# The down projection of an FFN as seven block products: two of three parts, weights in chunks of four k tiles, block sums moved to GpSimd

## The chip, the core and the metric

The kernel runs on one core of one Trainium2 chip. A time is the device time of one launch in microseconds (us); the smaller, the better. TensorE (PE) multiplies into PSUM, VectorE (DVE) and ScalarE (ACT) work on SBUF and PSUM, GpSimd (POOL) on SBUF, and SyncE (SP) issues the loads. The engines run side by side and wait for one another on semaphores.

## What is computed

A trunk of two layers on 512 tokens of width 1024, all in float32. Each layer has an FFN, a mixing part (three branches), and a second FFN; the change touches only the four FFNs.

```python
def swiglu(h, w_gate, w_up, w_down):
    return (jax.nn.silu(h @ w_gate) * (h @ w_up)) @ w_down
...
for i in range(DEPTH):        # DEPTH = 2, D_MODEL = 1024, D_FF = 2816, SEQ = 512
    x = x + 0.5 * swiglu(rms_norm(x, ffn1_norm[i]), ffn1_w_gate[i], ffn1_w_up[i], ffn1_w_down[i])
    ...                       # attention, gating and pooling branches, output projection
    x = x + 0.5 * swiglu(rms_norm(x, ffn2_norm[i]), ffn2_w_gate[i], ffn2_w_up[i], ffn2_w_down[i])
return rms_norm(x, final_norm)
```

## The kernel before

**Precision.** Each float32 operand is split into a rounded part "hi" (written by ACT) and the rest "lo" (written by DVE, a subtraction). A product is three matmuls: hi by hi, hi by lo, lo by hi.

**Units.** Weights come in units of 256 columns. A gate or up unit has the eight k tiles of D_MODEL. A plain unit is `columns`: 2 column halves by 8 k tiles by 3 matmuls, 48 matmuls of 512 tokens. Gate and up units alternate; two of them make a pair, which gives two k tiles of the activation. An FFN has 11 pairs, cut into three parts (`PART_PAIRS`): 3, 4 and 4 pairs. After the pairs of a part come its four down units (`D_PAIRS`), which multiply the part's activation by 256 columns of `w_down` and are added to the residual `xT`.

**Seven products.** In parts 2 and 3 a gate or up unit is `unit7`: token halves, weight column halves and k halves form 2 by 2 blocks, and seven products of block sums take the place of eight (Strassen's method in Winograd's form). Each product is 4 k tiles by 3 matmuls of 256 tokens, so a unit has 84 matmuls of 256. The sums of weight blocks (`t_sum`) are made by DVE in `t_sums`, ACT rounds them (`hi_t123`, `hi_rest`), DVE makes their lo parts (`lo_first`, `lo_rest`). The results of the seven products are joined by DVE from the PSUM tensors `psum` and `side` in three steps (four instructions). The six gate and up units of part 1 and all twelve down units are plain.

**Order.** Each engine runs a program written out by hand; the waits are on semaphores. PE works without a pause from unit to unit; ACT and DVE prepare the weights of one or two units ahead, between the evacuations. `act_lo_part` writes the lo part of a pair's activation, and PE waits for it pair by pair: the first down unit of a part has the last pair's two k tiles last (`need_act`).

## Time and profile before

| what | value |
|---|---|
| time, median of 3 runs | 2287.54 us (2286.88 to 2287.69) |
| span of the profiled execution, first to last instruction | 2285.9 us |
| median less span: what lies around the instructions | 1.6 us |
| PE busy | 100% of the span |
| DVE busy | 67% |
| ACT busy | 37% |
| GpSimd busy | 1% |
| mean granted TensorE clock | 0.999 of full speed |

The page gives busy time of each engine, the chain of work that ended last, and what an engine waited for. Matmuls are pipelined: one has a duration longer than the distance to the next, so their cost is read from the distance of starts. DVE and ACT durations include a fixed part that overlaps slightly with the next instruction.

### The profile page before, as it was taken

How to read it: one execution, taken by the hardware profiler on the slowest of the kernel's cores; microseconds unless marked ns; L12 is line 12 of the kernel's file. 1: busy time of each engine (PE TensorE's matmuls, PEld its weight loads, DVE VectorE, ACT ScalarE, POOL GpSimd, SP SyncE). 2: the span in 40 equal slices, each digit the busy share in tenths (PEclk: the TensorE clock that was granted, in tenths of full speed). 3: DMA queues.
4: the chain of work that ended last, by engine and by line, in shares of the span. 5: the costliest groups of instructions: out<-in, count | busy, mean ns of one | idle time of the engine just before them, and what ended most of it. 6: DMA issues, size and time to landing. Idle time of an engine off the chain costs nothing.

```text
span 2285.9 us, 31530 instructions
## 1 busy us (share of the span) xinstructions
PE 2275.0 (100%) x13549; PEld 1998.1 (87%) x13549; DVE 1529.1 (67%) x1721; ACT 849.6 (37%) x937; POOL 30.8 (1%) x70
## 2 busy tenths in 40 slices
PE   9999999999999999999999999999999999999998
PEld 7898998888888888989888989889888888899897
DVE  6895977455544568959668959665554355698694
ACT  5343433323522334424334434332244224344342
POOL 5000000000000000000000000000000000000000
PEclk9999999999999999999999999999999999999999
DMA  5324233322222423323223333332212333233232
GB/s 162 97 93 129 75 111 115 93 74 66 79 83 87 129 85 100 111 92 112 94 90 112 94 111 94 110 115 84 83 51 79 96 118 99 79 108 128 75 113 72
DMA packets 231393, 222.68 MB, mean 97 GB/s; under 512 B 4208, under 2 KB 229600, under 8 KB 231264
## 3 DMA queue, kind: packets, MB, share of 16 engines
q1 hardware_dynamic: 225744, 215.29, 30.0%
q10 hardware_dynamic: 5520, 5.51, 0.7%
q8 instruction: 100, 1.64, 0.3%
q14 instruction: 29, 0.24, 0.0%
HBM read 218.69 MB, written 2.10 MB: 97 GB/s over the span
## 4 chain that ended last, share of the span: by engine, by line
PE 99%; DVE 1%; ACT 0%; issue 0%; DVEq 0%; POOL 0%; POOLq 0%
PE psum L571 56%; PE psum L623 16%; PE side L623 12%; PE psum L837 6%; PE psum L771 2%; PE side L571 1%; PE psum L583 1%; PE side L894 1%; PE side L854 1%; PE side L874 0%; PE side L879 0%; PE side L781 0%; PE side L753 0%; PE side L862 0%; PE psum L698 0%; PE side L792 0%
## 5 line engine op out<-in xcount | busy, mean ns | idle before, releaser
L571 PE MATMUL psum<-h_hi,w_hi 128*128 128x512 f32 x944 | 369.5, 391 | 0.2 <-DVE wide L1446 0.2
L571 PE MATMUL psum<-h_hi,w_lo 128*128 128x512 f32 x944 | 367.4, 389 | 0.0
L571 PE MATMUL psum<-h_lo,w_hi 128*128 128x512 f32 x944 | 367.3, 389 | 0.0
L1424 DVE TENSOR_TENSOR w_lo<-raw,w_hi 128x2048 fp32r<-128x2048 f32 (+2 forms) x127 | 248.4, 1956 | 100.2 <-ACT w_hi L970 99.4
L970 ACT ACTIVATE w_hi<-raw 128x2048 fp32r<-128x2048 f32 (+2 forms) x127 | 208.6, 1642 | 246.9 <-PE psum L571 219.8
L623 PE MATMUL psum<-s_hi,hi 128*128 128x256 f32 x1024 | 289.8, 283 | 0.0
L623 PE MATMUL psum<-s_lo,hi 128*128 128x256 f32 x1024 | 289.8, 283 | 0.0
L571 PE MATMUL psum<-act_hi,w_lo 128*128 128x512 f32 x704 | 273.9, 389 | 0.0
L1068 ACT ACTIVATE hi<-t_sum 128x1536 fp32r<-128x1536 f32 (+1 forms) x128 | 134.2, 1055 | 264.7 <-DVE t_sum L1608 264.7
L571 PE MATMUL psum<-act_hi,w_hi 128*128 128x512 f32 x576 | 224.1, 389 | 0.0
L571 PE MATMUL psum<-act_lo,w_hi 128*128 128x512 f32 x576 | 224.1, 389 | 0.0
L623 PE MATMUL psum<-s_hi,t_lo 128*128 128x256 f32 x768 | 217.3, 283 | 0.0
L623 PE MATMUL side<-s_lo,hi 128*128 128x256 f32 x768 | 217.3, 283 | 0.0
L623 PE MATMUL side<-s_hi,hi 128*128 128x256 f32 x768 | 217.3, 283 | 0.0
L571 PEld LDWEIGHTS psum<-h_hi,w_hi 128*128 128x128 f32 x944 | 177.2, 188 | 37.8 <-issue 0.7
L571 PEld LDWEIGHTS psum<-h_lo,w_hi 128*128 128x128 f32 x944 | 177.2, 188 | 37.3 <-issue 0.7
L571 PEld LDWEIGHTS psum<-h_hi,w_lo 128*128 128x128 f32 x944 | 177.2, 188 | 36.8
L623 PEld LDWEIGHTS psum<-s_hi,hi 128*128 128x128 f32 x1024 | 196.6, 192 | 0.0
L623 PEld LDWEIGHTS psum<-s_lo,hi 128*128 128x128 f32 x1024 | 196.6, 192 | 0.0
L1489 DVE SCALAR_TENSOR_TENSOR xT<-psum,xT 128x1024 f32<-128x1024 f32 x53 | 64.9, 1224 | 139.6 <-PE psum L571 139.3
L571 PEld LDWEIGHTS psum<-act_hi,w_lo 128*128 128x128 f32 x704 | 132.1, 188 | 27.4
L623 PEld LDWEIGHTS side<-s_hi,hi 128*128 128x128 f32 x768 | 147.4, 192 | 0.3
(272 smaller groups left out, 4342.2 us busy)
## 6 DMA issues: line engine op xcount, KB each, us to landing
raw<-in_ffn_w_up_dram SPq DMA_DIRECT2D x44, 1024.0 KB, 5.4
raw<-in_ffn_w_gate_dram SPq DMA_DIRECT2D x43, 1024.0 KB, 5.4
raw<-in_w_in_dram SPq DMA_DIRECT2D x42, 1024.0 KB, 5.3
raw<-in_ffn_w_down_dram SPq DMA_DIRECT2D x32, 1024.0 KB, 5.2
raw<-in_ffn_w_down_dram SPq DMA_DIRECT2D x16, 768.0 KB, 4.5
raw<-in_w_in_dram SPq DMA_DIRECT2D x24, 512.0 KB, 4.2
raw<-in_w_out_dram SPq DMA_DIRECT2D x8, 1024.0 KB, 5.3
raw<-in_w_proj_b_dram SPq DMA_DIRECT2D x8, 512.0 KB, 3.5
```

The costliest lines, as they stand in the source:

```text
L571: mm = nc.tensor.matmul(dst[:, c * S:(c + 1) * S], l[:, a], r[:, b], start=first and k == ks[0] and n == 0, stop=last and k == ks[-1] and ...
L583: mm = nc.tensor.matmul(o, l[:, k * P:(k + 1) * P], r[:, k * S:(k + 1) * S], start=(k == 0 and n == 0), stop=(k == KD - 1 and n == 2))
L623: mm = nc.tensor.matmul(o[:, col:col + HALF], l(k), r[:, b], start=k == 0 and n == 0, stop=k == KH - 1 and n == 2)
L771: mm = nc.tensor.matmul(d, l[:, k * S + t * P:k * S + (t + 1) * P], r[:, b], start=(k == 0 and m == 0), stop=(k == KD - 1 and m == 2))
L837: mm = nc.tensor.matmul(psum[0][:, c * S:(c + 1) * S], l[:, k * UNIT_N + c * P:k * UNIT_N + (c + 1) * P], r[:, k * S:(k + 1) * S], start=( ...
L854: nc.tensor.matmul(outs[b][h * HQ:(h + 1) * HQ, col:col + k1 - k0], t[rows_of(b), q + h * HQ:q + (h + 1) * HQ], t[rows_of(b), k + k0:k + k ...
L894: mm = nc.tensor.matmul(side[1][rows_of(b), KEYS + q0:KEYS + q1], v[:, col:col + HEAD_DIM], pT[b][:, c0:c0 + q1 - q0], start=(m == 0), sto ...
L970: nc.scalar.activation(w_hi[s][:, 0:k * n], raw[s][:, 0:k * n], ACT.Copy).then_inc(hi_made, 1)
L1068: nc.scalar.activation(dst, src, ACT.Copy).then_inc(hi_made, 1)
L1424: nc.vector.tensor_tensor(w_lo[s][:, a], raw[s][:, a], w_hi[s][:, a].bitcast(F32), ALU.subtract).then_inc(split_made, 1)
L1489: i_ = nc.vector.scalar_tensor_tensor(x_, src, scale, x_, ALU.mult, ALU.add)
```

## The change

- The parts are 4, 4 and 3 pairs. The first six gate and up units stay plain. The other sixteen gate and up units and the eight down units of parts 1 and 2 are made as seven products (`seven`). The four down units of part 3 stay plain, now over six k tiles.
- The weights of a unit with seven products come in two chunks of four k tiles (512 KB each): 48 chunks an FFN, numbered 0 to 47. Chunks 0 to 3 are the last pair of part 1, 4 to 11 its down units, 12 to 27 the gate and up units of part 2, 28 to 35 its down units, 36 to 47 part 3. A chunk is 42 matmuls of 256 tokens; the second chunk of a unit adds to the first in PSUM. A down unit's two chunks stand in a row on PE: the first reads pairs 1 and 2 of the part, the second pairs 3 and 4.
- The block sums of the weights are made by GpSimd (`weight_sums`), two chunks ahead, behind the chunk that frees their buffer (three sets). GpSimd also makes the sums of the input (`input_sums`) and five of the eight block sums of a part's activation; DVE makes the last three (`act_sums`), when the last pair is there.
- DVE writes a pair's product into `ac_sum`; ACT rounds its seven blocks in groups, and DVE writes their lo parts in the same groups (`act_group`). PE waits for the three groups of pairs 1 and 2 before the first chunk of the first down unit, and for the three of pairs 3 and 4 before its second.
- A down unit is joined by DVE in four instructions and then added to `xT` from SBUF (before: one instruction from PSUM).

```diff
-    PART_PAIRS = ((0, 3), (3, 7), (7, 11))
-    PART_AT = (0, 10, 22)
+    PART_PAIRS = ((0, 4), (4, 8), (8, 11))
+    PART_AT = (0, 12, 24)
...
+    PLAIN = 6
...
+    CK = 4
+    CH = CK // 2
+    Q = CH * P
...
+            def weight_sums(f, q):
...
+                    after_chunk(pool, f, q - SETS)
+                after_loaded(pool, f, q)
+                t, b = t_sum[q % SETS], blocks(c_raw[q % RAWS])
+                nc.gpsimd.tensor_tensor(t[:, 0:2 * Q].rearrange("p (h k n) -> p h k n", h=2, n=P), b[:, :, :, 1, :],
+                                        b[:, 0].rearrange("p k c n -> p c k n"), ALU.subtract).then_inc(t_step, 1)
+                pool.wait_ge(t_step, 2 * (f * NC + q) + 1)
+                nc.gpsimd.tensor_tensor(tile7(t, T2_), tile7(t, T3_), b[:, 0, :, 0, :], ALU.add).then_inc(t_step, 1)
+                pool.wait_ge(t_step, 2 * (f * NC + q) + 2)
+                nc.gpsimd.tensor_tensor(tile7(t, T4_), b[:, 1, :, 0, :], tile7(t, T2_), ALU.subtract).then_inc(t_made, 1)
...
+            def seven(f, q, x_hi, x_lo, x_k, width, order):
...
+                pe.wait_ge(chunk_lo, 3 * (f * NC + q) + 2)
...
+                mm.then_inc(chunk_done if j == 0 else unit_done, 1)
...
+                for q, (n, j) in enumerate(CHUNKS):
...
+                    if down:
+                        if (n, j) == (PART_AT[p + 1] - D_PAIRS, 0):
+                            pe.wait_ge(ac_ready, 6 * (2 * f + p) + 3)
+                        if (n, j) == (PART_AT[p + 1] - D_PAIRS, 1):
+                            pe.wait_ge(ac_ready, 6 * (2 * f + p) + 6)
+                        seven(f, q, ac_hi[j], ac_lo[j], 0, CH, DOWN_ORDER)
...
+        LO_GROUPS = {0: ((0, 0, 0),), 1: ((0, 0, 1),), 2: ((0, 0, 2),), 4: ((0, 1, 0), (0, 1, 1), (0, 1, 2)),
+                     21: ((1, 0, 0),), 22: ((1, 0, 1),), 23: ((1, 0, 2),), 28: ((1, 1, 0), (1, 1, 1), (1, 1, 2))}
```

DVE's loop over the chunks, which sets the order of its work (`finish` joins the unit before; at the end of a part it also makes the product and the sums):

```diff
+                    pending = finish(*finished) if finished is not None else None
+                    finished = None
+                    if q + 2 < NC:
+                        chunk_lo_b(q + 2)
...
+                    if j == 1 and not down:
+                        dve.wait_ge(product_done, 6 * m + 3)
...
+                        take_first(m, s)
+                    if q + 2 < NC and j == 0:
+                        chunk_lo_t(q + 2)
+                    if j == 1 and not down:
+                        dve.wait_ge(product_done, 6 * m + 5)
+                        take_second(s)
+                    if q + 2 < NC and j == 1:
+                        chunk_lo_t(q + 2)
...
+                    for p_, j_, g_ in LO_GROUPS.get(q, ()):
+                        act_group(p_, j_, g_)
```

**DVE, behind the last up unit of a part.** Before, from the wait for the end of that unit (`unit_done`): joining, product, lo part, then the weights of the next down unit and its evacuation. L1576 is the lo part that PE waits for.

```order
L1670 TENSOR_TENSOR wide<-side,acc 128x512 [waits unit_done]
L1674 TENSOR_TENSOR wide<-wide 128x1024 [waits silu_made,side_evacuated1]
L1576 TENSOR_TENSOR act_lo<-wide,act_hi 128x1024 [waits act_hi_made]
L1636 TENSOR_TENSOR w_lo_57<-raw_74,w_hi_55 128x2048 [waits hi_made]
L1489 SCALAR_TENSOR_TENSOR xT<-psum,xT 128x1024 [waits unit_done]
```

Of the change, from the same wait: joining, product into `ac_sum`, three sums, the three lo instructions of the chunk after next (L1739, L1746, L1748), and the three groups (L1700) that PE waits for.

```order
L1777 TENSOR_TENSOR wide<-side,rstd 128x512 [waits unit_done]
L1675 TENSOR_TENSOR ac_sum_96<-wide 128x2x2x256 [waits silu_made,side_evacuated1]
L1685 TENSOR_TENSOR ac_sum_96<-ac_sum_96 128x512 [waits ac_pool,ac_made]
L1687 TENSOR_TENSOR ac_sum_96<-ac_sum_96 128x512 [waits ac_step]
L1689 TENSOR_TENSOR ac_sum_96<-ac_sum_96 128x512 [waits ac_step]
L1739 TENSOR_TENSOR c_raw_lo_80<-c_raw_75,c_hi_90 128x4x128 [waits chunk_hi,t_made]
L1746 TENSOR_TENSOR t_lo_87<-t_sum_84,c_hi_90 128x1024 [waits chunk_hi]
L1748 TENSOR_TENSOR c_raw_lo_80<-c_raw_75,c_hi_90 128x2x128
L1700 TENSOR_TENSOR ac_lo_98<-ac_sum_96,ac_hi_94 128x1024 [waits ac_hi_made,ac_summed]
L1700 TENSOR_TENSOR ac_lo_98<-ac_sum_96,ac_hi_94 128x1024 [waits ac_hi_made]
L1700 TENSOR_TENSOR ac_lo_98<-ac_sum_96,ac_hi_94 128x1536 [waits ac_hi_made]
```

Three instructions stood between the end of the unit and the last value that PE needs; now eleven do.

**PE, where it waits for the last pair of a part.** Before, in the first down unit of part 2, the wait for the last pair stands behind 36 of the unit's 48 matmuls.

```order
L571 MATMUL psum<-act_hi,w_lo_56 128x512
L571 MATMUL psum<-act_hi,hi_d 128x512 [waits act_ready]
L571 MATMUL psum<-act_lo,hi_d 128x512
```

Of the change, at the start of chunk 5, the second of the first down unit of part 1; the 42 matmuls of chunk 4 stand ahead of it.

```order
L764 MATMUL side<-ac_hi_93,c_raw_lo_83 128x256
L764 MATMUL side<-ac_hi_94,c_hi_92 128x256 [waits chunk_lo,ac_ready]
L764 MATMUL side<-ac_lo_98,c_hi_92 128x256
```

The wait moved from behind 36 matmuls of 512 to behind 42 of 256.

**GpSimd.** Before, it has after the masks of the start only two instructions in the whole program.

```order
L522 AFFINE_SELECT masks<-masks 128x128 [waits mask_step]
L530 AFFINE_SELECT w_sT<-w_sT 128x512 [waits side_evacuated1] x2
```

Of the change, the sums of chunks 2 and 3 and the one activation sum behind them: three instructions a chunk, each behind the one before, the first behind PE's end of an earlier chunk (`chunk_done` or `unit_done`).

```order
L618 TENSOR_TENSOR t_sum_86<-c_raw_76 128x512 [waits chunk_loaded2,split_made]
L621 TENSOR_TENSOR t_sum_86<-t_sum_86,c_raw_76 128x256 [waits t_step]
L623 TENSOR_TENSOR t_sum_86<-c_raw_76,t_sum_86 128x256 [waits t_step]
L618 TENSOR_TENSOR t_sum_84<-c_raw_77 128x512 [waits chunk_loaded3,chunk_done]
L621 TENSOR_TENSOR t_sum_84<-t_sum_84,c_raw_77 128x256 [waits t_step]
L623 TENSOR_TENSOR t_sum_84<-c_raw_77,t_sum_84 128x256 [waits t_step]
L630 TENSOR_TENSOR ac_sum_96<-ac_sum_96 128x512 [waits ac_made]
```

GpSimd had nothing to do in an FFN; now it has 144 such instructions for weights in each, and every chunk passes through it before ACT and DVE.

## Rows read from the trace of the kernel before

**Rows 1.** The page: span, then busy time, share and instructions of engines

```profile
span 2285.9 us, 31530 instructions
PE 2275.0 (100%) x13549; PEld 1998.1 (87%) x13549; DVE 1529.1 (67%) x1721; ACT 849.6 (37%) x937; POOL 30.8 (1%) x70
```

**Rows 2.** The page: the chain that ended last, by engine

```profile
PE 99%; DVE 1%; ACT 0%; issue 0%; DVEq 0%; POOL 0%; POOLq 0%
```

**Rows 3.** All waits of PE: for whom, us in total, times, longest

```profile
PE psum L698 <- POOL ident L487: 1.7, 1, 1.7
PE side L598 <- DVE acc L1769: 1.3, 1, 1.3
PE psum L571 <- DVE wide L1446: 0.2, 1, 0.2
```

**Rows 4.** The chain in order of time: start us, us, instructions merged

```profile
114.35 5.76 PE psum L623 x48
124.43 5.76 PE psum L623 x48
...
193.55 43.55 PE psum L571 x192
```

**Rows 5.** Groups of DVE by form: busy us, mean ns, idle before

```profile
L1620 DVE TENSOR_TENSOR t_lo<-t_sum,hi 128x1536 fp32r<-128x1536 f32 x64 | 112.1, 1752 | 0.0
...
L1608 DVE TENSOR_TENSOR t_sum<-t_sum,raw 128x512 f32<-128x512 f32 x64 | 44.3, 692 | 2.2
...
L1670 DVE TENSOR_TENSOR wide<-side,acc 128x512 f32<-128x512 f32 x64 | 44.2, 691 | 14.7 <-PE side L623 13.1
L1663 DVE TENSOR_TENSOR acc<-psum,wide 128x512 f32<-128x512 f32 x64 | 43.9, 687 | 10.9 <-PE psum L623 10.3
...
L1674 DVE TENSOR_TENSOR wide<-wide 128x1024 f32<-128x1024 f32 x32 | 39.2, 1226 | 1.1
...
L1664 DVE TENSOR_TENSOR wide<-psum,acc 128x256 f32<-128x256 f32 x64 | 27.2, 424 | 2.2
```

**Rows 6.** Timeline of DVE from 35 us: start us, us, instruction

```profile
35.17 2.35 DVE L1446 TENSOR_TENSOR wide<-psum,rstd 128x1024 f32<-128x1024 f32 x2
```

**Rows 7.** Timeline of GpSimd, the masks at the start: start us, us, instructions merged

```profile
19.41 2.95 POOL L516 TENSOR_SCALAR_AFFINE_SELECT masks<-masks 128x128 bf16<-128x128 bf16 x3
...
24.20 3.35 POOL L516 TENSOR_SCALAR_AFFINE_SELECT masks<-masks 128x128 bf16<-128x128 bf16 x3 [0.50 <-POOL masks L509]
...
34.01 1.09 POOL L516 TENSOR_SCALAR_AFFINE_SELECT masks<-masks 128x128 bf16<-128x128 bf16 x3
...
375.50 0.64 POOL L530 TENSOR_SCALAR_AFFINE_SELECT w_sT<-w_sT 128x512 f32<-128x512 f32 x1 [339.96 <-ACT w_sT L1237]
```

**Rows 8.** Timeline of DVE over the first two of these stretches

```profile
19.02 2.39 DVE L1424 TENSOR_TENSOR w_lo<-raw,w_hi 128x2048 fp32r<-128x2048 f32 x1 [0.56 <-ACT w_hi L970]
23.65 3.74 DVE L1768 TENSOR_TENSOR squares<-squares,squares 128x1024 f32<-128x1024 f32 x3 [2.24 <-ACT squares L991]
```

**Rows 9.** Lines L516 and L1424 alone: duration ns min/median/max

```profile
L516 POOL TENSOR_SCALAR_AFFINE_SELECT masks<-masks x12: 294/294/2152, 19.4 to 34.8; 128x128 bf16<-128x128 bf16 x12
...
L1424 DVE TENSOR_TENSOR w_lo<-raw,w_hi x127: 681/2291/2390, 19.0 to 2011.9; 128x2048 fp32r<-128x2048 f32 x83, 128x1024 fp32r<-128x1024 f32 x20, 128x1536 fp32r<-128x1536 f32 x16, 128x512 fp32r<-128x512 f32 x8
```

**Rows 10.** PE's last instructions, from the timeline

```profile
2277.60 0.60 PE L939 MATMUL psum<-ident,xT 128*128 128x128 f32 x4
```

**Rows 11.** Windows of the end: busy us of engines, PEclk, DMA share, GB/s

```profile
2279.00:2280.00 1.00, 0.00 (x0) 0.00 (x0) 1.00 (x2) 0.69 (x1) 0.00 (x0) 1.00 0.46 174
2280.00:2281.00 1.00, 0.00 (x0) 0.00 (x0) 1.00 (x2) 0.69 (x1) 0.00 (x0) 0.87 1.02 375
2281.00:2282.00 1.00, 0.00 (x0) 0.00 (x0) 0.21 (x1) 0.00 (x0) 0.00 (x0) 0.50 1.01 377
```

**Rows 12.** The page: issues of loads, KB each, median us from issue to landing

```profile
raw<-in_w_in_dram SPq DMA_DIRECT2D x24, 512.0 KB, 4.2
```

**Rows 13.** A group of ACT by form: busy us, mean ns, idle before

```profile
L1091 ACT ACTIVATE act_hi<-wide 128x1024 fp32r<-128x1024 f32 x32 | 34.0, 1061 | 89.7 <-DVE wide L1674 89.7
```

More of the change, by code:

```diff
@@ new lines, in act_sums @@
+            def act_sums(f, p, j, which):
+                t, made = ac_sum[j], 8 * f + 4 * p + 2 * j
+                for o, x1, x2, op, step in which:
+                    pool.wait_ge(ac_made, made + step)
+                    nc.gpsimd.tensor_tensor(quarter(t, o, 0, CH, CH), quarter(t, x1, 0, CH, CH), quarter(t, x2, 0, CH, CH),
+                                            op).then_inc(ac_pool, 1)
+                    act_sums.n += 1
+                    pool.wait_ge(ac_pool, act_sums.n)
+            act_sums.n = 0
@@ new lines, in need_act @@
+                def need_act(k):
+                    if k % 2 == 0:
+                        pe.wait_ge(act_ready, counts["act"].next())
+                for d in range(D_PAIRS):
+                    pe.wait_ge(split_made, counts["unit"].next())
+                    slot = DOWN_SLOTS[d]
+                    columns(begin(d % 2), (w_hi[slot], w_lo[slot]), act_hi, act_lo, range(DOWN_K[2][1] - DOWN_K[2][0]), True, True,
+                            need=need_act if d == 0 else None, halves=True).then_inc(unit_done, 1)
@@ L1047, in inner @@
                     counts["unit"].next()
[L1048 removed]
+                    if i < PLAIN // 2 - 1:
+                        split()
+                    else:
+                        chunk_hi_b(0)
+                        chunk_hi_t(0)
                     counts["unit"].next()
@@ L1101, in split_d, with down_split @@
+                def down_split(d):
+                    k = DOWN_K[2][1] - DOWN_K[2][0]
+                    r = DOWN_SLOTS[d]
+                    act.wait_ge(raw_loaded[r], counts[f"raw{r}"].next(16))
                     act.wait_ge(unit_done, counts["unit"].now(2))
                     a = slice(0, k * UNIT_N)
-                    hi(w[:, a], (raw7 if d == 1 else raw[r])[:, a])
-                for i in range(PART_PAIRS[0][1]):
+                    nc.scalar.activation(w_hi[r][:, a], raw[r][:, a], ACT.Copy).then_inc(hi_made, 1)
@@ new lines, in ffn @@
+                act.wait_ge(act_made, 3 * f + pending + 1)
+                nc.scalar.activation(pair(act_hi, pending), us[:, :], ACT.Copy).then_inc(act_hi_made, 1)
+                for d in range(D_PAIRS):
+                    if d < D_PAIRS - 1:
+                        down_split(d + 1)
+                    elif not last or layer < DEPTH - 1:
+                        split()
+                    counts["unit"].next()
+                    if last and layer == DEPTH - 1:
+                        last_residual(d, d % 2)
+                    else:
+                        residual(gain, d, d % 2)
@@ new lines, in ffn @@
+                    for p_, j_, g_ in LO_GROUPS.get(q, ()):
+                        act_group(p_, j_, g_)
+                    if j == 1:
+                        finished = ((n, p, i, down, s), m)
+                clear_acc()
+                act_lo_part(finish(*finished))
+                for d in range(D_PAIRS):
+                    if d < D_PAIRS - 1:
+                        down_split(d + 1)
+                    elif not last or layer < DEPTH - 1:
+                        split()
+                    if not (d == D_PAIRS - 1 and last and layer == DEPTH - 1):
+                        done()
+                    if last and layer == DEPTH - 1:
+                        last_residual(0.5, d, d % 2)
+                    else:
+                        residual(0.5, gain, d, d % 2)
```

743 lines of the change are left out of this document (378 added, 365 removed).

## Prediction

> **What bounds the kernel now.** I read the page first: PE is busy for the whole span of 2285.9 us, DVE for 67%, GpSimd for 1% [rows 1]. A busy PE alone proves nothing, so the chain of what ended last comes next: 99% of it is PE [rows 2]. The waits settle it: in the whole program PE waited three times, 3.2 us in all, and 0.2 us of that inside an FFN [rows 3]. So in the FFNs the time is the number of matmuls by their distance, and every wait that the change gives to PE is paid in full. The distances come from the chain in order of time. A unit of 84 matmuls of 256 tokens is followed 10.08 us later by the same place of the next: 120 ns a matmul. 192 matmuls of 512 tokens take 43.55 us: 226.8 ns a matmul [rows 4].
>
> **PE's own work.** A plain down unit over eight k tiles is 48 matmuls, 10.88 us; as seven products it is 84, 10.08 us: 0.80 us less, not an eighth, as a matmul of 256 costs more than half of one of 512. Per FFN the gate and up units stay as they are (six plain, sixteen of seven products). The down units had 22 k tiles by 4 units, 528 matmuls of 512; now they have 144 of those and 8 by 84 of 256. That is 384 by 226.8 ns (87.1 us) out, 672 by 120 ns (80.6 us) in: 6.4 us less an FFN, **25.6 us less** in four.
>
> **Where PE would wait: the second chunk of the first down unit.** Call T the end of the last up unit of a part. Before, PE had 36 matmuls of 512 (8.2 us) before it needed the last pair, and DVE needed three instructions. Now PE has one chunk, 42 by 120 ns = 5.04 us. DVE has in a row: joining 0.69, product 1.23, three sums 3 by 0.69, the lo parts of the chunk after next 0.69 + 1.23 + 0.42, the three groups 1.23 + 1.23 + 1.75 [rows 5]; there joining is L1670, the product and everything of 1024 is L1674, 512 from SBUF is L1608, 256 is L1664, 1536 is L1620. The sum is 10.5 us; instructions without a wait between them overlap by 0.1 us (two of 1.225 take 2.35 [rows 6]), which leaves 10.1. DVE isn't free at T either: it can take the fifth product only 12 matmuls before T (T - 1.44), the two instructions of that step last 0.69 + 0.42 (L1663, L1664), then L1746 and L1748 of another chunk follow (1.55), to T + 1.2. The groups are ready at T + 11.3: **PE waits 6.3 us** in part 2.
>
> In part 1 the same chain stands behind a backlog. DVE can't start on chunk 1 before the last plain unit ends (ACT's buffer for it waits for that). From there to the last group of pairs 3 and 4 it has 38 instructions: 13 of 1024 (15.9), 2 of 1536 (3.5), 9 of 512 in SBUF (6.2), 6 of 512 from PSUM (4.1), 8 of 256 (3.4), together 33.2, less about 20 overlaps of 0.1: 31.1 us. PE has five chunks, 25.2 us, ahead of its wait: **5.9 us** of waiting, if DVE never waits itself. The two make 12.2 us an FFN, 48.8 in four.
>
> **GpSimd against DVE.** The masks show what GpSimd does beside DVE. Three L516 take 1.09 us at 34.01, where DVE runs a reciprocal or reads PSUM, but 2.95 us at 19.41 and 3.35 us at 24.20 [rows 7]. There DVE runs instructions with two inputs in SBUF [rows 8]; one L516 took 2152 ns, not 294, and ended just behind DVE's, and that DVE instruction took 2390 ns, not the median 2291 [rows 9]. So the two take turns, whole instructions at a time, and the loser waits. Almost all that DVE does in a chunk has two inputs in SBUF, and so have all of GpSimd's sums. No row has GpSimd with two inputs. The nearest: one input of 512 float32 takes 0.64 us, of 128 elements 0.29, so 0.9 ns an element [rows 7, 9]. A chunk's sums have 1024 elements: 0.9 us of holding at that rate, 1.8 at twice it. I take the upper, as each element needs two operands, and 2.0 with the hand-overs. Behind T two chunks' sums fall into DVE's chain (one starts at T, one a chunk later): 4.0 us, less 0.7 beside joining, which reads PSUM: 3.3. In part 1 four chunks' sums and one of the activation do (8.9), of which DVE's nine instructions from PSUM and its waits for ACT can hide half: 4. Together 7.3 us an FFN, **29 in four**; from below 1.3 and 0 (5 in four), from above 5 and 8 (52).
>
> The Trainium skill (GPSIMD Engine Reference, Performance versus the Vector engine) measured a two-input add of 2048 float32 on GpSimd at 4497 ns, 2.2 ns an element; by that a chunk's sums hold 2.25 us instead of 1.8, and the sum would be some 7 us higher. No row of this trace can confirm it.
>
> **The clock.** PE's last matmul starts at about 2278 us [rows 10], and the granted clock is 1.00 until 2280, 0.87 in the next us, then 0.50, that is 1.2 instead of 2.4 GHz [rows 11]. So an idle PE has the lower level within about 2.5 us, and a wait of 9 us ends in it. No row shows the way back: between nothing and a whole chunk at half rate (5 us lost). I take 2 us, eight times: **16**.
>
> **What costs nothing.** Loads: 512 KB land in 4.2 us [rows 12], and a chunk is asked for two chunks ahead; so they stay hidden. Behind the last up unit of part 3 the cover shrinks to 24 matmuls, 5.4 us; DVE needs 0.69 + 1.23, ACT 1.06 [rows 13], DVE 1.23 again, some 4.5 with DVE free at T - 0.3: it just fits, and would cost what it lacks if DVE is late. In the steady stretches DVE has per chunk 2.4 us of lo parts, 1.3 of joining and up to 0.6 for products, GpSimd about 2.6, against 5.04: covered, with little to spare.
>
> **Sum.** The profiled span of 2285.9 and the 1.6 around it give the median of 2287.5. 2287.5 - 25.6 + 48.8 + 29 + 16 = **2356 us**, 3% slower.
>
> **The rivals.**
> - *The cover is enough* (faster). ACT and DVE have all but the last pair ready ahead, PE never waits, 2287.5 - 25.6 = 2262 us. For it: DVE has a third of its time free. Against: that third isn't behind T, where eleven instructions of 10.5 us stand against 5.04. It decides at the point where the last group ends before T + 5.04, which needs five microseconds of those instructions to be absent. Between it and the next, a total wait under 6.4 us an FFN would do. Chance 0.11, and 0.03 for landing at no change.
> - *Only DVE's chain* (slower, little). GpSimd's turns are short or fall into DVE's idle time, and the clock returns at once: 2287.5 - 25.6 + 48.8 = 2311, up to 2320. Chance 0.16.
> - *GpSimd and DVE fill every chunk.* DVE holds the SBUF inputs about 2.4 us a chunk, a quarter of a product (0.3) and in part 2 the groups; GpSimd 2.0. That is 4.7 of 5.04. If GpSimd's instructions cost half as much again, or each change of turns 0.1 us more, the loop needs 5.4 in all 192 chunks: 0.4 by 192 = 77 us on top, 2356 + 77 = 2433. For it: the doubled durations in rows 7. Against: PE stalls give slack back. The Trainium skill (SBUF — State Buffer, Who interferes with whom) has this as an exclusive lock for the whole instruction; the 2152 ns agree. Chance 0.12.
> - *As forecast*, 2320 to 2400: chance 0.58.
>
> **Numbers.** 2356. The low end is 48.8 and 5 for the turns with a free return of the clock, 2316, and some microseconds for instructions that I placed too late: 2306. The high end takes 52 for the turns and 40 for the clock: 2403. Outside are the fast rival and the saturated one. Slower by over 0.2% (4.6 us, about what a measurement can tell from no change) 0.86, same 0.03, faster 0.11.
>
> **What would show it.** The waits of PE in the changed kernel name L764 <- DVE `ac_lo` L1700, eight times, 6 to 13 us each, and little else. The lines of GpSimd show L618 over 1 us, with a spread up to DVE's durations. PEclk falls to half around these waits. The count of matmuls grows by 1152. The prediction is wrong if PE's waits for L1700 are under 3 us (then DVE gets there sooner than its rows say), or if they are small beside waits for `chunk_lo` (L1746, L1748) everywhere (then the turns decide), or if a matmul of 256 in `seven` isn't 120 ns apart.

## The result and the profile after

The changed kernel takes 2476.66 us (2476.28 to 2477.02, four runs) against 2287.31 us before: ratio 1.0828, 95% interval 1.0813 to 1.0844. It is 189 us slower; 2356 was forecast, with 2403 as the high end. The direction was right, the size was not, and the largest single term of the loss was one that the forecast had at nothing.

The page of the changed kernel: span, busy times, and the chain that ended last, by engine.

```profile
span 2474.7 us, 35503 instructions
...
PE 2302.9 (93%) x14701; PEld 2071.2 (84%) x14701; DVE 1811.4 (73%) x1945; ACT 958.7 (39%) x1253; POOL 900.4 (36%) x702
...
PE 64%; DVE 21%; issue 6%; POOL 5%; ACT 4%; DVEq 0%; POOLq 0%; ACTq 0%
```

Against [rows 1] and [rows 2]: 1152 matmuls more, as counted, but the chain is PE for 64% only, where it was 99%. All waits of PE (for whom, us in total, times, longest):

```profile
PE side L764 <- DVE ac_lo L1700: 93.9, 12, 11.5
PE side L764 <- DVE t_lo L1746: 65.5, 44, 3.2
PE psum L817 <- POOL ident L551: 1.7, 1, 1.7
PE side L726 <- DVE acc L1897: 1.0, 1, 1.0
PE psum L699 <- DVE wide L1553: 0.2, 1, 0.2
```

The first row is the wait that was forecast, twelve times instead of eight: twice in each FFN in the second chunk of a part's first down unit, and once more at chunk 4, where PE waits some 2 us for the groups of pairs 1 and 2. The second is the surprise: 44 waits of 3.2 us at most, for the lo part of a chunk's block sums. Before there were three waits in all [rows 3].

What the preparing engines take, groups by form (busy us, mean ns, idle before), first DVE and then GpSimd:

```profile
L1746 DVE TENSOR_TENSOR t_lo<-t_sum,c_hi 128x1024 fp32r<-128x1024 f32 x192 | 281.3, 1465 | 61.4 <-ACT c_hi L1197 61.4
L1739 DVE TENSOR_TENSOR c_raw_lo<-c_raw,c_hi 128x512 fp32r<-128x512 f32 x192 | 224.0, 1167 | 31.4 <-POOL t_sum L623 30.5 <-ACT c_hi L1193 0.8
...
L1748 DVE TENSOR_TENSOR c_raw_lo<-c_raw,c_hi 128x256 fp32r<-128x256 f32 x192 | 171.0, 891 | 0.0
L1772 DVE TENSOR_TENSOR rstd<-psum,wide 128x512 f32<-128x512 f32 x96 | 66.4, 692 | 6.5 <-PE psum L764 3.3
...
L618 POOL TENSOR_TENSOR t_sum<-c_raw 128x512 f32<-128x512 f32 x192 | 315.5, 1643 | 365.0 <-PE side L764 355.9 <-issue 7.2
L623 POOL TENSOR_TENSOR t_sum<-c_raw,t_sum 128x256 f32<-128x256 f32 x192 | 228.3, 1189 | 15.1
L621 POOL TENSOR_TENSOR t_sum<-t_sum,c_raw 128x256 f32<-128x256 f32 x192 | 200.3, 1043 | 15.1
```

DVE's three lo instructions of a chunk take 3.52 us in the mean, where DVE's instructions of 1024, 512 and 256 columns took 1.23, 0.69 and 0.42 before [rows 5]: 1.19 us more. The 512 columns that read PSUM, 692 ns, are no longer than before. GpSimd's three sums take 3.88 us.

Where the time goes in the first FFN, in five stretches: chunks 0 to 2, 3 to 6 (into the down units of part 1), 7 to 22, 23 to 30 (the same at part 2), 31 to 47. Windows of the changed kernel: length, then busy us of PE, PEld, DVE, ACT and GpSimd (instructions), PEclk, DMA share, GB/s.

```profile
80.80:98.90 18.10, 15.35 (x126) 15.14 (x126) 18.03 (x16) 10.36 (x15) 16.86 (x13) 1.00 0.36 113
98.90:136.70 37.80, 25.91 (x168) 25.54 (x169) 30.50 (x34) 12.63 (x18) 12.34 (x11) 0.78 0.14 44
136.70:223.20 86.50, 81.86 (x675) 80.87 (x673) 79.19 (x83) 35.74 (x59) 65.53 (x52) 1.00 0.36 104
223.20:284.20 61.00, 44.77 (x336) 43.85 (x337) 52.35 (x56) 23.87 (x35) 32.21 (x26) 0.89 0.19 61
284.20:374.90 90.70, 86.72 (x715) 85.77 (x714) 84.11 (x90) 37.51 (x60) 57.76 (x45) 1.00 0.31 94
```

Read the lengths against 5.04 us a chunk, which is 15.1, 20.2, 80.6, 40.3 and 85.7. The two stretches around a boundary lose 17.6 and 20.7 us, the three others 3.0, 5.9 and 5.0. Of the 3.0, 2.9 us are the wait that ends the stretch, before the first matmul of chunk 3, and of the 5.9, 3.3 us are the wait before chunk 23. In chunks 7 to 22 DVE is busy for 79.19 of 86.5 us: 4.95 us a chunk against PE's 5.04. DVE's 73% on the page is an average; here it has hardly any room left.

### The profile page after: what moved, and what is told of

It is laid out like the page before. It is cut to its first block, busy times and chain, and to the rows that moved or that the text cites. A ratio compares the mean times of both kernels' runs of the same rounds, so it can differ in the third digit from the quotient of the medians.

```text
span 2474.7 us, 35503 instructions
## 1 busy us (share of the span) xinstructions
PE 2302.9 (93%) x14701; PEld 2071.2 (84%) x14701; DVE 1811.4 (73%) x1945; ACT 958.7 (39%) x1253; POOL 900.4 (36%) x702
## 4 chain that ended last, share of the span: by engine, by line
PE 64%; DVE 21%; issue 6%; POOL 5%; ACT 4%; DVEq 0%; POOLq 0%; ACTq 0%
PE psum L699 36%; PE psum L764 9%; PE side L764 7%; DVE t_lo L1746 5%; PE psum L956 5%; DVE c_raw_lo L1739 3%; DVE c_raw_lo L1748 3%; DVE ac_lo L1700 3%; PE psum L890 2%; POOL t_sum L618 2%; DVE rstd L1772 2%; DVE wide L1767 1%; DVE wide L1777 1%; POOL t_sum L621 1%; ACT c_hi L1197 1%
## 5 line engine op out<-in xcount | busy, mean ns | idle before, releaser
L618 POOL TENSOR_TENSOR t_sum<-c_raw 128x512 f32<-128x512 f32 x192 | 315.5, 1643 | 365.0 <-PE side L764 355.9
L1746 DVE TENSOR_TENSOR t_lo<-t_sum,c_hi 128x1024 fp32r<-128x1024 f32 x192 | 281.3, 1465 | 61.4 <-ACT c_hi L1197 61.4
L1197 ACT ACTIVATE c_hi<-t_sum 128x1024 fp32r<-128x1024 f32 x192 | 202.4, 1054 | 318.1 <-POOL t_sum L623 317.8
L1531 DVE TENSOR_TENSOR w_lo<-raw,w_hi 128x2048 fp32r<-128x2048 f32 (+1 forms) x111 | 228.3, 2057 | 102.6 <-ACT w_hi L1090 102.3
L764 PE MATMUL psum<-s_hi,c_hi 128*128 128x256 f32 x1024 | 295.0, 288 | 0.0
L764 PE MATMUL psum<-s_lo,c_hi 128*128 128x256 f32 x1024 | 294.9, 288 | 0.0
L764 PE MATMUL side<-s_hi,c_hi 128*128 128x256 f32 x768 | 224.6, 292 | 66.7 <-DVE t_lo L1746 65.5
L1739 DVE TENSOR_TENSOR c_raw_lo<-c_raw,c_hi 128x512 fp32r<-128x512 f32 x192 | 224.0, 1167 | 31.4 <-POOL t_sum L623 30.5
L623 POOL TENSOR_TENSOR t_sum<-c_raw,t_sum 128x256 f32<-128x256 f32 x192 | 228.3, 1189 | 15.1
L764 PE MATMUL side<-s_lo,c_hi 128*128 128x256 f32 x768 | 218.7, 285 | 0.0
L621 POOL TENSOR_TENSOR t_sum<-t_sum,c_raw 128x256 f32<-128x256 f32 x192 | 200.3, 1043 | 15.1
L764 PE MATMUL side<-ac_hi,c_hi 128*128 128x256 f32 x384 | 115.2, 300 | 94.3 <-DVE ac_lo L1700 93.9
```

The lines of the kernel that those rows point to most:

```text
L618: nc.gpsimd.tensor_tensor(t[:, 0:2 * Q].rearrange("p (h k n) -> p h k n", h=2, n=P), b[:, :, :, 1, :], b[:, 0].rearrange("p k c n -> p c k ...
L621: nc.gpsimd.tensor_tensor(tile7(t, T2_), tile7(t, T3_), b[:, 0, :, 0, :], ALU.add).then_inc(t_step, 1)
L623: nc.gpsimd.tensor_tensor(tile7(t, T4_), b[:, 1, :, 0, :], tile7(t, T2_), ALU.subtract).then_inc(t_made, 1)
L764: mm = nc.tensor.matmul(outs[side_][:, col:col + HALF], l, r[:, a], start=j == 0 and bank not in cleared, stop=j == 1 and k == CH - 1 and ...
L1197: nc.scalar.activation(c_hi[q % SETS][:, 0:4 * Q], t_sum[q % SETS][:, :], ACT.Copy).then_inc(chunk_hi, 1)
L1531: nc.vector.tensor_tensor(w_lo[s][:, a], raw[s][:, a], w_hi[s][:, a].bitcast(F32), ALU.subtract).then_inc(split_made, 1)
```

## The experiments

All times are compared with 2476.7 (the changed kernel) and 2287.4 to 2287.5 (before, in each group of runs). A time without a ratio or a range is that of a single run. Where GpSimd's weight sums are replaced, the block sums aren't computed.

### Take GpSimd's sums away

**w_short** and **w_long**: memsets, which read nothing, in place of the three sums.

```diff
-                nc.gpsimd.tensor_tensor(t[:, 0:2 * Q].rearrange("p (h k n) -> p h k n", h=2, n=P), b[:, :, :, 1, :],
-                                        b[:, 0].rearrange("p k c n -> p c k n"), ALU.subtract).then_inc(t_step, 1)
+                nc.gpsimd.memset(t[:, :], 1.0).then_inc(t_step, 1)
...
-                nc.gpsimd.tensor_tensor(tile7(t, T2_), tile7(t, T3_), b[:, 0, :, 0, :], ALU.add).then_inc(t_step, 1)
+                nc.gpsimd.memset(t[:, 0:1], 1.0).then_inc(t_step, 1)     # w_long: t[:, :]
...
-                nc.gpsimd.tensor_tensor(tile7(t, T4_), b[:, 1, :, 0, :], tile7(t, T2_), ALU.subtract).then_inc(t_made, 1)
+                nc.gpsimd.memset(t[:, 0:1], 1.0).then_inc(t_made, 1)     # w_long: t[:, :]
```

> GpSimd's three weight sums of a chunk are left out: in their place it writes constants, 1024 columns once and one column twice, and reads nothing (the output is not the reference's). Theory of turns (GpSimd and VectorE take turns at instructions that read SBUF, and GpSimd's 2.7 us a chunk lengthens VectorE's): VectorE's L1746, L1739 and L1748 return to 1.22, 0.69 and 0.42 us, the waits for chunk_lo in the steady stretches vanish, and the two waits of a part's first down unit shrink to about 6 us each: 2287.5 - 25.6 + 49 + 16 for the clock, 2315 to 2345 us. Rival, latency (the sums simply come too late to ScalarE and VectorE): also near 2330, as the sums are short here.

Measured: 2349.9, a little above the range.

> As the run before, but GpSimd writes 1024 columns of constants three times a chunk, about 2.9 us, as long as its real sums last when nothing disturbs them (2.7 us), still without reading SBUF. Theory of turns: as the short one, 2315 to 2350 us, with VectorE's lo parts at their lone durations. Rival, latency: the sums' length is what delays the chain, so 2430 to 2480 us, as the changed kernel.

Measured: 2364.1, 14 us over the range of the turns and 66 under that of the rival. So 127 of the 189 us go with the sums, and most of them even where GpSimd is busy 2.9 us a chunk, so long as it reads nothing. What is left has the forecast shape. Windows of w_short over the stretches 3 to 6, 7 to 22 and 23 to 30:

```profile
95.60:128.10 32.50, 22.53 (x170) 22.15 (x169) 25.54 (x33) 12.73 (x18) 4.60 (x12) 0.84 0.21 65
128.10:208.80 80.70, 80.70 (x675) 80.70 (x674) 63.67 (x85) 36.75 (x59) 24.77 (x52) 1.00 0.36 105
208.80:258.40 49.60, 42.19 (x337) 41.81 (x337) 41.19 (x54) 24.20 (x35) 10.87 (x25) 0.93 0.28 86
```

The steady stretch is at PE's pace, 80.7 us, and DVE has 3.98 us a chunk. The stretches around the boundaries still lose 12.3 and 9.3 us. In PE's timeline the waits (18.0) and slower matmuls (3.7) of an FFN add up to 21.7 us here, 86.8 in four; 2349.9 less that is 2263.1. So **PE's own work is what was forecast, 2262**.

### Give the sums to DVE, or share them

**sums_on_dve** moves the three sums into DVE's program, ahead of the lo parts of the same chunk.

```diff
                     if q + 2 < NC:
+                        weight_sums(q + 2)       # on DVE; none on GpSimd
                         chunk_lo_b(q + 2)
```

> The weights' block sums of every chunk are made by VectorE itself (0.69 + 0.42 + 0.42 us a chunk), all else as in the changed kernel. Theory of turns: GpSimd's 2.7 us a chunk cost VectorE more than making the sums would; VectorE then has about 5.1 us of work in a chunk of 5.04, so it is just full: 2262 + 60 for the two boundaries + 16 for the clock + 20 to 40, 2350 to 2385 us, faster than the changed kernel by 4 to 5%, still slower than before. Rival (VectorE's load decides, and GpSimd took work off it): slower than the changed kernel, above 2490 us.

Measured: 2511.2, ratio 1.0979 (1.0961 to 1.0998): worse than the change, and my expectation was wrong. The rival was right. Groups of DVE by form show why:

```profile
L1755 DVE TENSOR_TENSOR t_lo<-t_sum,c_hi 128x1024 fp32r<-128x1024 f32 x192 | 234.6, 1222 | 51.8 <-ACT c_hi L1193 51.7
...
L1748 DVE TENSOR_TENSOR c_raw_lo<-c_raw,c_hi 128x512 fp32r<-128x512 f32 x192 | 136.7, 712 | 6.3
L1738 DVE TENSOR_TENSOR t_sum<-c_raw 128x512 f32<-128x512 f32 x192 | 131.3, 684 | 0.0
L1740 DVE TENSOR_TENSOR t_sum<-t_sum,c_raw 128x256 f32<-128x256 f32 x192 | 97.2, 507 | 6.7
L1741 DVE TENSOR_TENSOR t_sum<-c_raw,t_sum 128x256 f32<-128x256 f32 x192 | 85.5, 445 | 6.6
```

The lo parts are back at 1222 and 712 ns, and so the 1.19 us are gone, but the sums bring 0.684 + 0.507 + 0.445 = 1.64 us. The order also has a gap, since the sums that ACT rounds are made just before: in the stretch below DVE waits 0.4 us for ACT (start us, us, instruction, idle before). Over all chunks these gaps add up to 51.8 us; the changed kernel has 61.4 at the same instruction, so they don't explain the difference.

```profile
156.48 0.68 DVE L1738 TENSOR_TENSOR t_sum<-c_raw 128x512 f32<-128x512 f32 x1
...
158.12 0.69 DVE L1748 TENSOR_TENSOR c_raw_lo<-c_raw,c_hi 128x512 fp32r<-128x512 f32 x1
159.21 1.23 DVE L1755 TENSOR_TENSOR t_lo<-t_sum,c_hi 128x1024 fp32r<-128x1024 f32 x1 [0.40 <-ACT c_hi L1193]
...
160.69 0.69 DVE L1738 TENSOR_TENSOR t_sum<-c_raw 128x512 f32<-128x512 f32 x1
```

From L1738 to the next L1738 it is 4.21 us for a chunk, before any joining of products. The window of chunks 7 to 22 has DVE busy 86.49 of 92.8 us, 5.41 a chunk, over PE's 5.04:

```profile
133.60:226.40 92.80, 84.97 (x675) 83.89 (x674) 86.49 (x131) 36.35 (x60) 5.90 (x4) 0.96 0.32 91
```

**sums_shared** leaves the sum of 512 on GpSimd and gives DVE the two of 256.

```diff
+                        rest_sums(q + 2)         # DVE: T2 and T4; GpSimd: T3 and T1 only
                         chunk_lo_b(q + 2)
```

> The changed kernel, but of a chunk's three sums GpSimd makes only the first (512 columns), and DVE the two of 256 ones, ahead of the chunk's lo parts, all computed. Until the sums are ready it now takes GpSimd about 1.5 us and DVE 0.95, where it took GpSimd 3.88. If GpSimd's lateness were the cause, this is a gain of 30 to 60 us: 2415 to 2445. If the sum of DVE's work decides: it gets 0.95 us more in each chunk and loses about half of the 1.19 us of lengthening, so its three lo instructions and sums take about 3.8 us where they took 3.52 (and 3.97 where DVE made all sums, 2511): 2485 to 2505.

Measured: 2531.7, ratio 1.1070 (1.1051 to 1.1088), above both guesses. Freeing GpSimd of half its sums gains nothing; it has the added DVE work and still a part of the lengthening. DVE's total on the page goes the same way in these three kernels, which compute everything: busy 1811.4, 1863.6 and 1883.9 us for 2476.7, 2511.2 and 2531.7. It is no measure by itself: the kernels with another order, below, have the changed kernel's total and are faster.

### Change the order

**two_first** runs the first two down units after a part as first, first, second, second chunk; **groups_first** puts the act groups of pairs 3 and 4 ahead of the next chunk's sums on ACT and DVE.

```diff
-            CHUNKS += [(n + d, j) for d in range(D_PAIRS) for j in range(2)]
+            CHUNKS += [(n, 0), (n + 1, 0), (n, 1), (n + 1, 1)]
+            CHUNKS += [(n + d, j) for d in range(2, D_PAIRS) for j in range(2)]
```
```diff
+                    if q in (4, 28):             # on DVE; on ACT ahead of chunk_hi_t in the same way
+                        for p_, j_, g_ in LO_GROUPS[q]:
+                            act_group(p_, j_, g_)
                     if q + 2 < NC:
                         chunk_lo_b(q + 2)
```

> The first chunks of a part's first two down units stand ahead of their second ones, so TensorE has 10.08 us instead of 5.04 before it needs pairs 3 and 4. If the boundary chain is VectorE's work behind the last up unit, each of the eight waits there shrinks by 5 us: 40 us less, 2430 to 2440 us. If that chain is fed by something that also moves (GpSimd's or ScalarE's work for later chunks), the gain is under 20 us.

Measured: 2458.6, ratio 1.0746 (1.0728 to 1.0764): 18 us, not 40, and so under the 20 of the second guess. PE's waits for `ac_lo` fell from 93.9 to 69.9 us only.

> At the two boundaries ScalarE and VectorE make the three groups of pairs 3 and 4 before the parts of the chunk after next, instead of behind them. In the changed kernel L1739, L1746 and L1748 stand there with 3.5 us in the mean (2.3 alone). If the boundary waits are this chain in VectorE's order, they shrink by 2.3 to 3.5 us each, 18 to 28 us in all: 2448 to 2460 us. If they are set by the three sums or by GpSimd, nothing changes: 2477 us.

Measured: 2460.2, ratio 1.0759 (1.0741 to 1.0777): 16 us, at the lower edge of the first guess. DVE has the same total in it, 1811.9 us.

**all_three** is these two edits and the sums on DVE; **both_orders** is the two edits alone, and **short_both_orders** has the memsets of w_short besides.

> Sums on VectorE, two first chunks ahead, and the groups first, together. If the three costs are separate and add up: 2365 less 40 for the cover less 18 for the order, about 2305 to 2325 us, near the kernel before. If VectorE's load is the bound in the steady stretches, the boundary gains are partly eaten there: 2330 to 2360 us.

Measured: 2484.5, ratio 1.0862 (1.0844 to 1.0881). A miss by over 120 us; it has the sums on DVE, which cost more than the orders gave, and against **sums_on_dve** the two orders are worth 27 us.

> The changed kernel with both reorderings of before together: the first two down units after a part take turns by chunks (their first chunks, then their second), and at that place ACT and DVE round the act groups before the weight sums of the chunk two ahead. Each alone took 18 and 16 us off 2476.7. If the two shorten different waits, about 2442. If both only let DVE's queue be shorter at the same place (that DVE has as much to do there as TensorE is what is waited for, whatever the order), 2448 to 2462: a reordering removes no DVE work.

Measured: 2451.2 (2444.8 to 2456.8), ratio 1.0724 (1.0706 to 1.0742): 25 of the 34 that they gave apart. The four runs are 12 us apart, so that the 25 is less certain than the figures of the other kernels.

> As both_orders, and GpSimd's three sums of a weight chunk are replaced by one memset of the chunk's 1024 columns and two of one column, as in w_short: the weights' block sums are not computed. w_short alone took 2349.9, with 21.7 us in each FFN (87 in all) of wait and lowered clock, nearly all of it at the two boundaries after a part; without that 87 it would be 2263, the 25.6 us under the kernel before that TensorE's products should save. If the boundary's wait is the act groups standing late in DVE's queue, the two reorderings now help more, as DVE has room: 2285 to 2315. If the wait there is DVE's own amount of work, 2325 to 2345.

Measured: 2304.2. With GpSimd's reads gone the same two edits are worth 46 us, with them 25. So at a boundary the order is worth more once DVE has room. From the distances of PE's matmuls the loss is then 42 us in four FFNs; 2304.2 - 42 is again 2262.

### Separate DVE's length from GpSimd's

**t_lo_set** keeps GpSimd's sums and makes `t_lo` a memset on DVE. **more_dve_work** and **some_dve_work** are w_short with three or two additions of 256 columns of constants a chunk. **gpsimd_long** has four memsets on GpSimd, **gpsimd_long_dve_more** those and DVE's three additions. **hi_in_halves** is the real kernel with ACT's rounding of the sums cut in two.

```diff
-                    nc.vector.tensor_tensor(t_lo[q % SETS][:, :], t_sum[q % SETS][:, :], w[:, 0:4 * Q].bitcast(F32),
-                                            ALU.subtract).then_inc(chunk_lo, 1)
+                    nc.vector.memset(t_lo[q % SETS][:, :].bitcast(F32), 0.0).then_inc(chunk_lo, 1)      # t_lo_set
```
```diff
+                    more = [nc.vector.tensor_tensor(spare[i]..., some, some, ALU.add) for i in range(3)]   # more_dve_work
```
```diff
+                    act.wait_ge(t_step, 2 * (f * NC + q) + 1)                                           # hi_in_halves
+                    nc.scalar.activation(c_hi[q % SETS][:, 0:2 * Q], t_sum[q % SETS][:, 0:2 * Q], ACT.Copy)
                     act.wait_ge(t_made, f * NC + q + 1)
-                    nc.scalar.activation(c_hi[q % SETS][:, 0:4 * Q], t_sum[q % SETS][:, :], ACT.Copy).then_inc(chunk_hi, 1)
+                    nc.scalar.activation(c_hi[q % SETS][:, 2 * Q:4 * Q], t_sum[q % SETS][:, 2 * Q:4 * Q], ACT.Copy).then_inc(chunk_hi, 1)
```

> The changed kernel, GpSimd's weight sums as they are, but DVE's t_lo (the fp32r remainder of a chunk's four sums, 1024 columns, a subtraction of 1.47 us in the mean) is a memset to zero of the same columns, which reads nothing: the remainders of the weights' sums are left out. If what TensorE waits for is the amount of DVE's work in a chunk (3.52 us in the three lo instructions, of it 1.19 us lengthening beside GpSimd), this takes away 0.4 to 1.2 us of it in every chunk (a memset of these columns may take 0.3 to 1.1 us): 2370 to 2430. If it is GpSimd's sums coming late (its three take 3.88 us in the mean, and ACT waits 318 us for them), the time stays over 2450.

Measured: 2403.5. That is 73 us less, though GpSimd still takes 3.8 us a chunk. DVE's memset took 0.91 us. Window over chunks 7 to 22:

```profile
131.90:213.40 81.50, 80.79 (x675) 80.58 (x673) 57.16 (x83) 36.21 (x59) 62.42 (x52) 1.00 0.36 104
```

With GpSimd's sums in place and reading, but DVE busy for 3.6 us a chunk, this stretch is within 0.8 us of PE's pace. The loss is around the boundaries: 35 us an FFN from the distances of PE's matmuls.

> As w_short (GpSimd sets the weights' sums by a memset and two columns, and is busy only 377 us in all; the block sums are not computed; 2349.9 us), but DVE does three more additions of 256 columns into unused memory after the first lo part of each chunk (43 of the 48 chunks of each FFN), a little over 1.1 us a chunk: about what DVE's three lo instructions are longer by beside GpSimd in the changed kernel (1.19 us). DVE's busy time then goes from 1577 to about 1780 to 1795 us, where the changed kernel has 1811. If the length of DVE's work is what costs, whoever lengthens it: 2430 to 2475. If it is that the sums come late from GpSimd, which is not so here: under 2380.

Measured: 2394.0. A miss: the added length costs 44 us, not 80 to 125. DVE's busy time grew to 1751.9, less than planned, as the three additions overlap and take 1.09 us together.

> As more_dve_work with two additions a chunk instead of three, about 0.75 us a chunk, DVE busy about 1715 us. If DVE's work costs in proportion, two thirds of the difference of more_dve_work to w_short: 2405 to 2430. If there is slack that the first part of it fills (DVE is idle a third of the time in w_short), less than half of the difference: 2365 to 2400.

Measured: 2378.4, 28 of the 44: two thirds, in proportion to the work added, as the first guess has it. The time lies in the range of the second because the 44 was smaller than thought.

> GpSimd's three weight sums of a chunk are replaced by four memsets of the chunk's 1024 columns, which read nothing and take 3.9 us together, as long as the sums in the changed kernel; the block sums are not computed, and DVE's instructions stay at their own length. w_long with three (2.9 us) took 2364.1, w_short with one 2349.9. If GpSimd's lateness costs by itself as in t_lo_set (2403.5), 2385 to 2410; if it costs only with DVE's length, under 2380.

Measured: 2371.0. GpSimd as late as in the changed kernel costs 21 us. This run is the nearest to the changed kernel that has no reads: GpSimd's instructions for a chunk last 3.82 us against 3.88, and DVE's program is the same. **So 106 of the 189 us (2476.7 less 2371.0) come from GpSimd reading instead of only writing.**

> As gpsimd_long, and DVE does the three additions of 256 columns a chunk of more_dve_work (1.07 us a chunk). So both engines take as long for a chunk as in the changed kernel, with no turns taken between them; the block sums are not computed. If the round of a chunk's buffers is what is too long (GpSimd 3.9 us, ACT 1.05, DVE's lo parts 3.5 beside ACT, its joining of products 2.5, some 10 us against 10.1 between two chunks), the two together cost more than their sum, and it comes near the changed kernel: 2450 to 2480. If they only add up, 2350 + 44 + what gpsimd_long has over 2350: 2415 to 2445. If the port does something more, the lower end or under it.

Measured: 2418.2. Both together cost 68, near 44 + 21. They add up; the theory of a buffer's round that is too long, with more than the sum, finds no support.

> The changed kernel, all computed, but ACT rounds a chunk's four sums in two instructions of 512 columns, the first when GpSimd's first sum is there, beside its other two, where one of 1024 (1.04 us) waited for all three. After the last sum ACT then takes about 0.6 us. If the round of a chunk's buffers is too long in the steady stretches, 0.4 us less of it is worth up to 0.4 us at each chunk that waits (some 12 of 48 in each FFN), with the clock that comes back after the shorter waits: 10 to 30 us, 2447 to 2467. If DVE's amount of work alone sets the pace, nothing: 2472 to 2480.

Measured: 2473.2 (2473.2 to 2474.1), ratio 1.0813 (1.0795 to 1.0831): 3.4 us for 0.4 us less in the round, where that theory expected 10 to 30.

The third stretch (chunks 7 to 22) of more_dve_work and of gpsimd_long_dve_more:

```profile
131.50:212.20 80.70, 80.70 (x675) 80.70 (x674) 78.20 (x131) 36.92 (x59) 24.46 (x52) 1.00 0.36 105
```
```profile
131.00:216.10 85.10, 81.14 (x674) 80.67 (x672) 78.51 (x131) 35.93 (x60) 67.25 (x69) 1.00 0.36 104
```

In the first, with DVE busy 4.89 us a chunk and all inputs early, PE never waits: a DVE that is 97% full can still be hidden. With the same DVE and GpSimd busy 67 us, 4.4 us are lost, nearly all at the starts of chunks 22 and 23. The changed kernel has 79.19 and 65.53 and loses 5.9.

What remains between 2418.2 and 2476.7 is 58 us. In it DVE's busy time goes from 1755.0 to 1811.4, 56 us more: the three additions stand only in 43 of an FFN's 48 chunks (20 chunks by 1.2 is 24 us), and in the changed kernel GpSimd's reads lengthen DVE's other two-input instructions as well. Two forms in the changed kernel, and the same in gpsimd_long_dve_more:

```profile
L1700 DVE TENSOR_TENSOR ac_lo<-ac_sum,ac_hi 128x1024 fp32r<-128x1024 f32 x32 | 51.9, 1641 | 0.0
L1800 DVE SCALAR_TENSOR_TENSOR xT<-wide,xT 128x1024 f32<-128x1024 f32 x32 | 47.0, 1468 | 1.1
```
```profile
L1809 DVE SCALAR_TENSOR_TENSOR xT<-wide,xT 128x1024 f32<-128x1024 f32 x32 | 39.2, 1226 | 1.1
...
L1703 DVE TENSOR_TENSOR ac_lo<-ac_sum,ac_hi 128x1024 fp32r<-128x1024 f32 x32 | 38.3, 1218 | 0.0
```

That these 56 us of DVE work are the 58 us of time is argued from the equal size, and not shown by a run of its own. The same argument fails elsewhere: **t_lo_set** and **gpsimd_long** have almost the same totals (DVE busy 1587.4 and 1576.7 us, GpSimd 884.2 and 890.0), and yet t_lo_set takes 33 us more. With GpSimd's reads its `ac_lo` groups of 1024 columns take 1600 ns instead of 1218, and PE waits 86.2 us for them instead of 70.9. So it matters which of DVE's instructions are lengthened. That GpSimd's turns fall unevenly on the chunks may be a part of the 58 us; these runs can't separate it.

## Why the prediction was wrong

**Right: PE's own work, -25.6.** Two runs come to it: 2349.9 - 86.8 = 2263 and 2304.2 - 42 = 2262. 120 ns a matmul of 256 held.

**Nearly right: the wait in the second chunk after a part.** PE's timeline in the first FFN (start us, us, instruction, idle before), at the second chunk of the first down unit of both parts:

```profile
124.25 0.58 PE L764 MATMUL side<-ac_hi,c_hi 128*128 128x256 f32 x1 [9.92 <-DVE ac_lo L1700]
...
272.33 0.58 PE L764 MATMUL side<-ac_hi,c_hi 128*128 128x256 f32 x1 [11.48 <-DVE ac_lo L1700]
```

From start to start of the matmuls, less 0.12 each, these are 10.1 and 11.6 us, 21.7 an FFN (in the third FFN 19.2), where DVE's chain (12.2) and GpSimd's turns (7.3) made 19.5. That the sum came so near is in part luck, as the split was less good: w_short, with few reads left on GpSimd, has 8.6 and 7.4 us there, 16.0, so the chain is 3.8 us longer than I counted and the turns are 5.7. DVE's timeline before the first of the two waits ends shows both, without a gap:

```profile
114.16 0.69 DVE L1685 TENSOR_TENSOR ac_sum<-ac_sum 128x512 f32<-128x512 f32 x1
114.88 1.64 DVE L1687 TENSOR_TENSOR ac_sum<-ac_sum 128x512 f32<-128x512 f32 x1
116.56 1.09 DVE L1689 TENSOR_TENSOR ac_sum<-ac_sum 128x512 f32<-128x512 f32 x1
117.57 1.21 DVE L1739 TENSOR_TENSOR c_raw_lo<-c_raw,c_hi 128x512 fp32r<-128x512 f32 x1
118.71 1.21 DVE L1746 TENSOR_TENSOR t_lo<-t_sum,c_hi 128x1024 fp32r<-128x1024 f32 x1
119.84 0.41 DVE L1748 TENSOR_TENSOR c_raw_lo<-c_raw,c_hi 128x256 fp32r<-128x256 f32 x1
120.17 4.02 DVE L1700 TENSOR_TENSOR ac_lo<-ac_sum,ac_hi 128x1024 fp32r<-128x1024 f32 x3
```

L1687, L1689 and L1739 have 512 columns like L1685 and take 1.64, 1.09 and 1.21 instead of 0.69, and just then GpSimd makes the sums of a chunk:

```profile
114.41 1.56 POOL L618 TENSOR_TENSOR t_sum<-c_raw 128x512 f32<-128x512 f32 x1 [3.99 <-PE side L764]
116.05 1.05 POOL L621 TENSOR_TENSOR t_sum<-t_sum,c_raw 128x256 f32<-128x256 f32 x1
117.18 1.05 POOL L623 TENSOR_TENSOR t_sum<-c_raw,t_sum 128x256 f32<-128x256 f32 x1
```

**Right: the clock, 2 us a boundary.** Windows over the end of the first of the waits and behind it (PEclk is the third number from the end):

```profile
120.00:124.00 4.00, 0.00 (x0) 0.00 (x0) 4.00 (x4) 0.00 (x0) 0.00 (x0) 0.50 0.00 0
124.00:126.00 2.00, 1.75 (x8) 1.76 (x9) 0.79 (x2) 0.07 (x1) 0.00 (x0) 0.50 0.00 0
126.00:128.00 2.00, 2.00 (x11) 2.00 (x11) 0.70 (x1) 1.27 (x2) 0.00 (x0) 0.50 0.05 8
128.00:130.00 2.00, 2.00 (x14) 2.00 (x13) 0.86 (x2) 0.00 (x0) 0.00 (x0) 0.63 0.00 0
130.00:132.00 2.00, 2.00 (x19) 2.00 (x18) 0.13 (x1) 0.13 (x1) 0.09 (x1) 1.00 0.00 0
```

The level falls to 0.50 (1.2 GHz) in the wait and is 1.00 again some 5 us after PE resumes. In between a matmul of 256 is 0.21 us from the next, not 0.12. PE's timeline gives 2.4 and 1.8 us for the two boundaries, and 16 us for the eight in four FFNs, as forecast.

**Wrong: "covered, with little to spare", costed at 0.** This is the step that failed: outside the two boundary waits the prediction gave PE no wait at all. From PE's timeline, the distances of matmuls in all 48 chunks less 0.12 us each, an FFN loses 53.4 us in the mean. The two boundary waits with the clock behind them are 25.9 of it (22.9 in the third FFN). That leaves 28.3 an FFN, 113 in four, where the forecast had 0: some 22 of the 28.3 are waits, the rest is the clock behind them. With 6.5 us in four FFNs too little at the boundaries, that is 120 of the 121 us missed.

Only a third of the 113 us lies in stretches that the words "steady" describe. By chunks, the first FFN loses 1.0 us in chunks 0 to 2, 2.5 in 7 to 22 and 5.2 in 31 to 47, together 8.7. The other 18.6 lie in chunks 3 and 4 (8.0) and 23 to 28 (10.6), where DVE has the groups of the activation, too. Two of those waits:

```profile
98.93 0.58 PE L764 MATMUL side<-s_hi,c_hi 128*128 128x256 f32 x1 [2.78 <-DVE t_lo L1746]
...
223.20 0.39 PE L764 MATMUL side<-s_hi,c_hi 128*128 128x256 f32 x1 [3.15 <-DVE t_lo L1746]
```

The step failed in what it added up. DVE was counted at its own length of 2.4 us of lo parts, though the same prediction had DVE and GpSimd take turns. It charged the turns only at the boundaries, but they come with every chunk's sums and lengthen the lo parts to 3.52 us. The groups stand in DVE's program behind chunks 0 to 2 and 21 to 23 (`LO_GROUPS`), 4.2 us at their own length, and weren't in the sum for a chunk. GpSimd was counted at 2.6 us a chunk, and its weight sums alone take 3.88. With 1.24 of joining, the products and the groups, DVE reaches 4.95 of 5.04 us in the mean of chunks 7 to 22, and a chunk with a group in it is over (3.52 + 1.24 + 1.23 is 6.0). The runs bear out that it is the length of DVE's work: without the sums' reads (w_short) all three plain stretches are at PE's pace, and with the reads but lo parts of 2.24 us a chunk (t_lo_set) chunks 7 to 22 are within 0.8 us of it. That the groups are what tips chunks 3, 4 and 23 to 28 is read from the order of the program; no run takes them away by themselves. The rows for it were there ([rows 5], [rows 7]). The rule I should have followed: an engine that takes turns pays in every stretch where the other works, not only where it is waited for.

**The price of GpSimd's sums was too low.** I took 1.8 us a chunk from one-input rows. The sums of 512 and 256 columns take 1261 and 723 ns at the least, that is 2.1 ns an element and 0.19 us fixed, 2.71 us for the three without DVE in the way. What the prediction cited from the Trainium skill (GPSIMD Engine Reference, Performance versus the Vector engine) was nearer with 2.2 ns an element: an estimate of 2.25 us by its figure. A measured time for the very operation was a better neighbour than a row for another operation.

**The rivals.** "GpSimd and DVE fill every chunk" named the mechanism of the missing term and was nearest with 2433, but its shape was not what happened. It had 5.4 us in all 192 chunks, 77 us. Chunks 7 to 22 take 5.20 us each in the first FFN (86.5 less the wait before chunk 23, by 16), and the plain stretches of four FFNs lose some 34 us; the larger part, some 79, is in the uneven chunks. I gave it 0.12 because PE's stalls would give slack back. They don't at a boundary, since DVE works through that stall without a gap, as its timeline above shows.

## What to carry to other kernels

Before work moves to a second engine on the same SBUF inputs, write down for the bounding engine's smallest repeated piece (here a chunk of 5.04 us) what each helper does in it, with durations as they are beside one another. A helper that is at 79% of the piece alone (3.98 of 5.04 us) is at 98% with the other's turns, and then a chunk with more work than the mean becomes a wait. Removing the turns by giving the work back isn't a remedy if the work is longer than the turns cost (1.64 against 1.19 us). Here 0.8 us of PE a down unit was bought with 11 us of DVE (7.0 of lo parts, 2.5 of joining, 1.5 for the residual), where the plain unit had 3.5 (2.29 for the lo part, L1636, and 1.22 for the residual, L1489), and with 7.8 of GpSimd; even with the sums gone for nothing and the better order the kernel only came within 17 us of the one before.
